# Conformer-convolution and latent-attention trunk on one core: the running sums of two shared channel tiles move from GpSimd additions to accumulating DMAs, issued between the weight splits

## The reference

```python
def conformer_conv_branch(h, w_in, b_in, conv_w, conv_b, norm_g, norm_b, w_out, b_out):
    proj = h @ w_in + b_in                       # 1024 -> 3 x 2048
    val, glu_gate, z = jnp.split(proj, 3, axis=-1)
    u = val * jax.nn.sigmoid(glu_gate)
    u = lax.conv_general_dilated(                # 31 taps, causal, one filter per channel
        u, conv_w[:, None, :], window_strides=(1,), padding=[(CONV_KERNEL - 1, 0)],
        dimension_numbers=('NWC', 'WIO', 'NWC'), feature_group_count=CONV_WIDTH) + conv_b
    u = jax.nn.silu(layer_norm(u, norm_g, norm_b))   # mean and variance over all 2048 channels
    u = u * jax.nn.silu(z)
    return u @ w_out + b_out
...
h = layer_norm(alpha * h + conformer_conv_branch(...))     # layer A
h = layer_norm(alpha * h + mla_branch(...))                # layer B, 16 heads
```

## Time and profile before

| | before |
|---|---|
| time, median of 3 runs | 821.93 us (821.65 to 823.95) |
| the profiled execution's own time | 820.67 us |
| its span, first to last instruction | 818.7 us |
| TensorE busy | 807.0 us, 99% |
| VectorE busy | 602.9 us, 74% |
| GpSimd busy | 542.3 us, 66% |
| ScalarE busy | 395.5 us, 48% |
| mean granted TensorE clock | 0.999 of full speed |

### The profile page before, as it was taken

One profiled execution on the slowest core, in us unless ns is written; L12 is line 12 of the kernel. 1 busy time (PEld: TensorE's weight loads), 2 busy tenths in 40 slices (PEclk: granted clock), 3 DMA queues, 4 the chain that ended last, 5 costly groups with the idle time before them and its releaser, 6 DMA issues.

```text
span 818.7 us, 11442 instructions
## 1 busy us (share of the span) xinstructions
PE 807.0 (99%) x3891; PEld 681.3 (83%) x3891; DVE 602.9 (74%) x1026; ACT 395.5 (48%) x711; POOL 542.3 (66%) x335
## 2 busy tenths in 40 slices
PE   8999999999999999999999999999999999999996
PEld 8888888888888887888898788888888888888885
DVE  2699999999999978994833192037788888876217
ACT  4654444455564368622342444256666766664210
POOL 4677999995999954594355438426877776387430
PEclk9999999999999999999999999999999999999999
DMA  6333333330032324444233335115766664663412
GB/s 221 103 103 103 92 88 87 93 104 26 25 105 84 109 79 146 157 160 129 52 107 114 101 102 167 54 41 176 206 200 191 201 199 130 186 205 129 155 52 102
DMA packets 123019, 100.01 MB, mean 122 GB/s; under 512 B 15354, under 2 KB 107616, under 8 KB 122972
## 3 DMA queue, kind: packets, MB, share of 16 engines
q1 hardware_dynamic: 122972, 99.42, 40.4%
HBM read 82.36 MB, written 12.58 MB: 116 GB/s over the span
## 4 chain that ended last, share of the span: by engine, by line
PE 95%; DMA 2%; DVE 1%; ACT 0%; issue 0%; SPq 0%; DVEq 0%
PE bank L1694 91%; DMA x_in<-in_x_dram 1%; PE bank L1999 1%; PE bank L2000 1%; DMA prob_kept<-prob 1%; DMA prob_moved<-prob_kept 0%; PE bank L1873 0%; PE bank L1992 0%; DVE prob L1591 0%; PE bank L1926 0%; PE bank L1990 0%; PE bank L1808 0%; DVE prob L1596 0%; SPq L524 0%; ACT bank L1201 0%
## 5 line engine op out<-in xcount | busy, mean ns | idle before, releaser
L730 POOL TENSOR_TENSOR w_lo<-w_raw,w_hi 128x1024 fp32r<-128x1024 f32 x102 | 252.6, 2485 | 114.1 <-ACT w_hi L927 106.8
L1330 DVE SCALAR_TENSOR_TENSOR bank<-u,conv_w,bank 128x512 f32<-128x512 f32 x357 | 238.6, 747 | 0.5
L1694 PE MATMUL bank<-xt_hi,w_lo 128*128 128x512 f32 (+1 forms) x392 | 151.9, 388 | 0.0
L1694 PE MATMUL bank<-xt_hi,w_hi 128*128 128x512 f32 (+1 forms) x392 | 150.9, 385 | 0.0
L927 ACT ACTIVATE w_hi<-w_raw 128x1024 fp32r<-128x1024 f32 x102 | 106.3, 1054 | 92.2 <-PE bank L1694 29.8
L1694 PE MATMUL bank<-xt_lo,w_hi 128*128 128x512 f32 (+1 forms) x392 | 150.8, 385 | 0.0
L1694 PEld LDWEIGHTS bank<-xt_lo,w_hi 128*128 128x128 f32 x392 | 73.7, 188 | 15.0 <-issue 0.5
L1694 PEld LDWEIGHTS bank<-xt_hi,w_lo 128*128 128x128 f32 x392 | 73.7, 188 | 15.0 <-issue 0.5
L1694 PEld LDWEIGHTS bank<-xt_hi,w_hi 128*128 128x128 f32 x392 | 73.6, 188 | 14.7
L767 POOL TENSOR_TENSOR acc<-acc,tap_product 128x512 f32<-128x512 f32 x60 | 77.8, 1297 | 9.7 <-ACT tap_product L960 4.5
L1694 PE MATMUL bank<-ht_hi,w_lo 128*128 128x512 f32 (+1 forms) x208 | 76.4, 367 | 0.0
(11 more groups left out here) (213 smaller groups left out, 1722.0 us busy)
## 6 DMA issues: line engine op xcount, KB each, us to landing
w_raw<-in_a_w_in_dram SPq DMA_DIRECT2D x48, 512.0 KB, 3.7
w_raw<-in_b_w_in_dram SPq DMA_DIRECT2D x20, 512.0 KB, 3.6
prob_kept<-prob SPq DMA_DIRECT2D x16, 640.0 KB, 3.1
prob_moved<-prob_kept SPq DMA_DIRECT2D x64, 160.0 KB, 3.2
w_raw<-in_a_w_out_dram SPq DMA_DIRECT2D x16, 512.0 KB, 4.0
w_raw<-in_b_w_out_dram SPq DMA_DIRECT2D x16, 512.0 KB, 3.5
bundle_raw<-in_b_w_uq_dram SPq DMA_DIRECT2D x16, 256.0 KB, 4.4
x_in<-in_x_dram SPq DMA_DIRECT2D x4, 512.0 KB, 5.8
```

What stands on the lines that cost most here:

```text
L730: nc.gpsimd.tensor_tensor(w_lo[slot][:], w_raw[raw][:], w_hi[slot][:].bitcast(F32), ALU.subtract).then_inc(w_lo_ready, 1)
L1330: nc.vector.scalar_tensor_tensor(out=inner[:] if k < TAPS - 1 else acc[:, t, :], in0=u[:, t, k:k + SEQ], scalar=conv_w[:, column:column + ...
L1694: last = nc.tensor.matmul(out_ap, a, b, start=(start and n == 0 and m == 0), stop=(stop and n == len(parts) - 1 and m == 2))
```

## The change

The addition `acc += tap_product` by a GpSimd instruction becomes a DMA that GpSimd issues and that adds to its destination (`accum_op`). It counts 16 on its semaphore when it has landed, so every wait on `product_added` is multiplied by 16; the waits themselves stay, on both engines. In addition the taps are spread: in a value-gate round the first tap comes behind the first split, the second behind the second split, the third stays at the round's end; in a z column the first of the two taps comes ahead of the split. The last group between the matrices is 6 taps instead of 9, so that the z taps reach to z9 instead of z8. In `POOL_SUM` the two shared tiles go from the second and third place to the end.

```diff
-        PAIR_SHARE, MATRIX_SHARE, Z_SHARE = 3, (1, 1, 1, 9), 2
+        PAIR_SHARE, MATRIX_SHARE, Z_SHARE = 3, (1, 1, 1, 6), 2
-        POOL_SUM = MATRIX_TILES[1:] + SHARED_TILES + VECTOR_TILES[:8]
+        POOL_SUM = MATRIX_TILES[1:] + VECTOR_TILES[:8] + SHARED_TILES
 # GpSimd
             def value_gate(t):
+                taps = list(pair_taps(t))
                 for w in range(2):
                     if t == w == 0:
                         first_lo()
                     else:
                         split_lo(2 * t + w, w, (2 * t + w) % SLOTS)
+                    for n in taps[w:w + 1]:
+                        add_product(n)
...
-                for n in pair_taps(t):
+                for n in taps[2:]:
                     add_product(n)
...
                 pool.wait_ge(product_ready, n + 1)
-                wait(pool, product_added, added_before(n))
-                nc.gpsimd.tensor_tensor(acc[:, t, :], acc[:, t, :], tap_product[n % 2][:], ALU.add
-                                        ).then_inc(product_added, 1)
+                wait(pool, product_added, 16 * added_before(n))
+                nc.gpsimd.dma_start(acc[:, t, :], tap_product[n % 2][:], accum_op=ALU.add).then_inc(product_added, 16)
...
             for i in range(CT):
+                if i > 0:
+                    for n in list(z_taps(i))[:1]:
+                        add_product(n)
                 split_lo(Z0 + i, i % 2, i % SLOTS)
...
-                for n in z_taps(i):
+                for n in list(z_taps(i))[1 if i > 0 else 0:]:
                     add_product(n)
 # ScalarE: value_gate and the z loop spread tap_times_u in the same way around split_hi
-                    wait(act, product_added, added_before(n - 1))
+                    wait(act, product_added, 16 * added_before(n - 1))
```

More of the change, by code:

```diff
@@ L812, in sum_tiles @@
                         else:
-                            pool.wait_ge(product_added, added_before(len(shared_taps)))
+                            pool.wait_ge(product_added, 16 * added_before(len(shared_taps)))
                     wait(pool, pool_csum_done, n)
@@ L939, in value_gate @@
             def value_gate(t):
+                taps = list(pair_taps(t))
                 for w in range(2):
                     split_hi(2 * t + w, w, (2 * t + w) % SLOTS, 16 * (t + 1))
+                    for n in taps[w:w + 1]:
+                        tap_times_u(n)
                 keep_value_gate(t - 1, (t - 1) % ROUND)
```

## The result

The changed kernel takes 889.72 us (median of 4 runs, 889.18 to 891.03) against 822.94 us for the kernel before (4 runs, 821.65 to 824.63): a ratio of 1.083, 95% interval 1.080 to 1.086. It is slower by 67 us. The direction and the two kinds of wait were forecast; the size was not. A loss of 30 us was forecast (852 for the median), and 67 us were measured. 889.72 lies inside the whole stated range of 828 to 905, but above C's own range of 838 to 861.

What follows compares the result with a forecast made beforehand. TensorE was taken as the bound, with no slack behind layer A. Value-gate stage and weights cost 0, the chain to the mean 30.1 us: 820.67 + 30.1 = 850.8, so 852 us for a median, range 828 to 905.

Steps and rivals of the forecast that it cites:

- C: The forecast case: L from 3.0 to 4.0 us, time 838 to 861 us, 852 at 3.7; chance 0.42.
- TensorE is the bound, so relief is worth 0: All through layer A TensorE is the bound, so removing 82 us of GpSimd additions gains 0.
- L: Time from one chained DMA's issue to the next when nothing else holds GpSimd: 3.7 us, range 2.0 to 5.1.
- d: Time that one DMA issue holds GpSimd itself: taken as 1.0 us, between 0.41 and about 1.3.
- Weights. ... Cost 0: Weight loads, started two columns ahead, still land in time beside the 256 KB adds: cost 0.
- Value-gate stage. Cost 0.: Three adds per 10.88 us round fit up to L = 3.63; at 3.7 slack holds the 0.2 us lost: cost 0.
- From the matrices to the mean: Chain of adds through the z columns, then tile sums for csum: z9 24.2 us late, the mean 30.1 us late.
- nine in a row: Nine consecutive DMAs after the matrices, n = 36 to 44: first at 203.95, the last 8L later (29.6 us).
- D: Long chain, L over 4.0 us, unbroken from its first add at 69.14: 890 us at L = 4.5; chance 0.23.
- A: Not slower: the chain fits, with L up to 2.2 us losing under 2.5 us; time 822; chance 0.12.
- B: Short chain, L from 2.2 to 3.0 us: TensorE waits 2 to 16 us at z columns and mean; chance 0.17.
- E: Z stage: idle gaps lower TensorE's clock, so ten columns cost 35 us more, 887 us; chance 0.04.

Runs made afterwards that it cites:

- hybrid: Changed kernel with DMAs only for taps not issued as a load starts, the other additions GpSimd instructions again: 823.40 us, ratio 1.002.
- new order without DMAs: Changed kernel's order of taps, splits and tile sums, with all additions as GpSimd instructions as before: 821.48 us, ratio 1.001.
- half adds: Changed kernel with each accumulating DMA on 256 of the 512 positions: 867.95 us, ratio 1.056.
- small loads: Changed kernel with weight loads of 64 KB in place of 512 KB from the second group of four value-gate rounds on and in the z stage: 857.16 us.
- copies: Changed kernel with the 60 DMAs copying instead of adding: 837.55 us, ratio 1.019.
- filler matmuls: Changed kernel with 12 extra matmuls of 512 columns ahead of each of the columns z1 to z11: 889.01 us, ratio 1.085.

## Why the prediction was right in kind and wrong in size

**TensorE is the bound, so relief is worth 0.** Right. The hybrid and the new order without DMAs both stand at the time of before.

**One DMA costs L = 3.7 us, d = 1.0 us.** Right for a DMA by itself (3.77 and 0.87 us), and in part by luck. L was taken from the 3.7 us in which a 512 KB load lands. A landing is not yet an L: the add lands after 3.20 us, and 0.5 us more pass before the next one starts. And an add doesn't cost what its bytes would at the rate of loads: 2.5 us of it are fixed, by the half adds.

**"Weights. ... Cost 0", and with it one L for all stretches.** This is the step that failed. I asked only whether the adds would make the loads late. They hardly do (3.8 us to landing, 3.7 before). I did not ask whether the loads make the adds late, and there is no slack in the adds. In a value-gate round one add in three, and in a z column one in two, begins with a load and lands after 5.1 us in place of 3.2, so the next one starts 5.6 us after it. The Trainium skill, "DMA: Bandwidth & Descriptors", section "Issuing engines are not separate DMA queues", has the rule that I passed over: transfers issued by different engines run on the same 16 DMA engines and interleave. The packets above and the runs with 64, 256 and 512 KB loads agree with it.

**"Value-gate stage. Cost 0."** It failed in the main by the same step. The limit of 3.63 us per add was right, but a round takes 13.2 us in place of 10.88, 4.4 an add, and the first of the nine comes 21.2 us late. A small part would have come without the loads: L was 3.75 and not 3.7, the slack did not hold it, and with small loads 3.2 us of the 21.2 remain.

**From the matrices to the mean.** The structure held: z1 to z9 and then `csum`, in that order. The nine in a row and the last 24.1 us came within 0.5 us of their terms. The z columns' term was 59.2 us and measured 75.3, 16.1 more, again for the loads: two adds took 9.4 us and not 7.4.

**The signs.** GpSimd's busy time was to fall by some 80 us and fell by 23 (542.3 to 518.9). That was an error within the forecast, which had itself put d at 1.0 us: the 60 issues hold GpSimd for 0.87 us each, 52 us in all. The waits of TensorE ahead of z columns were to be some 2 us and are up to 4.0, after 9.3 ahead of z1; the one for `csum` is 4.5 us where 6 were expected.

**The rivals.** The numbers are nearest to D, with 0.23: waits on `w_lo` in the value-gate stage, and 890 at L = 4.5. The match is luck in part. D needed L over 4.0 and an unbroken chain; L in the nine in a row was 3.77, for which D's formula gives 847, and once, for 12.0 us, the chain was broken. What lengthened it is not what I had given for it (a slow descriptor writer, slow transfers), but the loads. A and B fall: in the changed kernel no two adds were less than 3.73 us apart. The Trainium skill's fit for a copy ("DMA: Bandwidth & Descriptors", section "Anatomy of one DMA — SWDGE (gpsimd) path"), 2.6 us for 256 KB as an estimate, lies between the copies' landing of 2.24 us and their distance of 2.8; it does not speak of additions, which took 3.75. E, with 0.04, had the effect and not the price: where TensorE waited ahead of the z columns the granted clock was 0.84 to 0.87 in the mean. It was to cost 35 us. In the z columns the filler matmuls show that it cost nothing; in the value-gate stage it may have cost up to 2 us.

**What stays open.** That it is the load which delays the add, and more so the larger it is, is shown, and so is that the add's packets start later, by 1.1 us in the case shown. Why the engines serve the load's packets first was not measured; that a transfer whose first packet comes ahead of the load's gets through, as the copies do, is read from two runs and not tested by shifting the issue.

## What to carry to other kernels

A DMA that must wait for the one before it has the price of a whole landing, here 3.75 us for work that the engine does in 1.37. Moving such a chain off an engine frees that engine only if the chain's length, landings included, fits the time of the engine that is the bound, and if nothing that the bounding engine needs is queued behind the waits. When a new transfer shares a stretch with periodic loads, ask both questions: what it does to the loads, and what they do to it; the one without slack is the one to cost. And start by asking what the relief could buy at all: TensorE had no wait in this stretch that a freer GpSimd would have shortened, so it was nothing.

## What the hardware showed that I had not expected

A GpSimd DMA that accumulates 256 KB within SBUF: 3.20 us to landing, 0.5 us until the next instruction that waited for it starts, 0.87 us of GpSimd. The same as a copy: 2.8 us in all and 0.54 us of GpSimd. One that starts with a 512 KB load: 5.1 us to landing, and as long for an add of 128 KB. TensorE's granted clock was 0.84 to 0.87 in the stretches with gaps between z columns, and with 12 filler matmuls per column it was 1.00 from 280 us on. VectorE made no difference that the rows show: in the changed kernel the distance over a split is 3.75 us both while VectorE is busy without a break (264.54 to 268.29) and while it waits for `pool_csum` (302.40 to 306.15).
